# Sixty-four bytes ahead of the weights' slots, other places for act_hi and act_lo, and one buffer less

## What is computed

```python
hx = modulate(rms_norm(x, g_mix_pre), sh1, sc1)              # and hc, of the context
uf, ux, ug = split(hx @ w_in)                                # 1024 + 1024 + 1024
y = concat([fourier_mix(uf), (h_f + h_b) * gelu(ug)]) @ w_out   # h_f, h_b: gated scans over conv(ux)
x = x + gt1 * rms_norm(y, g_mix_post)
hx2 = modulate(rms_norm(x, g_ffn_pre), sh2, sc2)
up = depthwise_conv(hx2 @ w_up)                              # 2048 -> 2 * 5632
g, v = split(up)
x = x + gt2 * rms_norm((gelu(g) * v) @ w_down, g_ffn_post)
```

## Time and profile before

| | |
|---|---|
| median of 3 runs | 2106.05 us (2105.69 to 2107.88) |
| profiled execution, its own time | 2105.41 us |
| span of its trace | 2103.6 us |
| PE busy | 2071.2 us, 98% |
| granted TensorE clock, mean of the span | 0.996 |

### The profile page before, as it was taken

The page is one execution under the profiler, slowest core; times in us unless marked ns, Lnnn a source line. Parts: engine busy times, 40 slices in busy tenths (PEclk is TensorE's granted clock), DMA queues, the critical chain, the costliest instruction groups (busy, mean ns, idle before and its releaser), DMA issues.

```text
span 2103.6 us, 28297 instructions
## 1 busy us (share of the span) xinstructions
PE 2071.2 (98%) x11682; PEld 1772.5 (84%) x11682; DVE 1529.6 (73%) x2202; ACT 811.6 (39%) x1077; POOL 78.7 (4%) x145
## 2 busy tenths in 40 slices
PE   7999999999999999999999999999999999999998
PEld 4678887888777888888889898898988889888887
DVE  5567978876988975867767676676766758577577
ACT  5346577543323442423324233332333424233243
POOL 0000000001110000000000000000000000000002
PEclk9999999999999999999999999999999999999999
DMA  9953424434876523333333333334233333232343
GB/s 394 408 204 110 154 96 161 137 109 173 323 277 225 181 90 134 100 128 111 110 130 101 138 103 103 129 101 140 100 120 121 100 130 100 91 101 101 100 172 109
DMA packets 86193, 311.19 MB, mean 148 GB/s; under 512 B 9456, under 2 KB 13552, under 8 KB 84016
## 3 DMA queue, kind: packets, MB, share of 16 engines
q1 hardware_dynamic: 67824, 243.09, 32.7%
q0 software_dynamic: 17424, 65.50, 9.1%
q10 hardware_dynamic: 816, 0.79, 0.1%
HBM read 300.95 MB, written 8.39 MB: 147 GB/s over the span
## 4 chain that ended last, share of the span: by engine, by line
PE 80%; DVE 2%; ACT 1%; DMA 1%; issue 0%; DVEq 0%; ACTq 0%
PE bank L988 26%; PE bank L990 26%; PE bank L989 26%; DMA w_raw<-in_stream 1%; PE bank L1099 1%; DVE acc L2167 0%; PE bank L1284 0%; DVE w_lo L1532 0%; ACT w_hi L602 0%; PE bank L1313 0%; PE bank L1194 0%; DVE acc L2139 0%; ACT lru_u L698 0%; DVE cv L1544 0%; DVE x L2193 0%
## 5 line engine op out<-in xcount | busy, mean ns | idle before, releaser
L988 PE MATMUL bank<-h_hi,w_hi 128*128 128x512 f32 (+1 forms) x1968 | 711.2, 361 | 4.2 <-ACT y_lru L671 1.2
L989 PE MATMUL bank<-h_lo,w_hi 128*128 128x512 f32 (+1 forms) x1968 | 708.6, 360 | 0.0
L990 PE MATMUL bank<-h_hi,w_lo 128*128 128x512 f32 (+1 forms) x1968 | 707.2, 359 | 0.0
L1532 DVE TENSOR_TENSOR w_lo<-w_raw,w_hi 128x1024 fp32r<-128x1024 f32 x260 | 316.0, 1222 | 157.9 <-ACT w_hi L602 157.8
L988 PEld LDWEIGHTS bank<-h_hi,w_hi 128*128 128x128 f32 x1968 | 372.3, 189 | 63.6 <-issue 11.9
L602 ACT ACTIVATE w_hi<-w_raw 128x1024 fp32r<-128x1024 f32 x260 | 273.0, 1056 | 389.1 <-DMA w_raw<-in_stream 389.0
L990 PEld LDWEIGHTS bank<-h_hi,w_lo 128*128 128x128 f32 x1968 | 372.1, 189 | 56.6
L989 PEld LDWEIGHTS bank<-h_lo,w_hi 128*128 128x128 f32 x1968 | 372.3, 189 | 49.0
L988 PE MATMUL bank<-act_hi,w_hi 128*128 128x512 f32 (+1 forms) x688 | 265.0, 385 | 1.7 <-DVE acc L2139 1.5
L990 PE MATMUL bank<-act_hi,w_lo 128*128 128x512 f32 (+1 forms) x688 | 264.2, 384 | 0.0
L989 PE MATMUL bank<-act_lo,w_hi 128*128 128x512 f32 (+1 forms) x688 | 264.2, 384 | 0.0
(11 more groups left out here) (340 smaller groups left out, 2711.4 us busy)
## 6 DMA issues: line engine op xcount, KB each, us to landing
w_raw<-in_stream SPq DMA_DIRECT2D x340, 512.0 KB, 3.5
ada_raw<-in_adabg POOLq DMA_DIRECT2D x112, 512.0 KB, 4.3
ada_raw<-in_ada SPq DMA_DIRECT2D x64, 512.0 KB, 13.5
x<-in_x_t SPq DMA_DIRECT2D x4, 1024.0 KB, 8.4
acc<-in_adabg SPq DMA_DIRECT2D x8, 512.0 KB, 6.1
x<-in_x_t POOLq DMA_DIRECT2D x4, 1024.0 KB, 9.4
x_kept_d<-x SPq DMA_DIRECT2D x4, 1024.0 KB, 5.6
c<-in_ctx_t SPq DMA_DIRECT2D x2, 1024.0 KB, 14.3
```

The lines of the kernel that those rows point to most:

```text
L988: t.matmul(out, w, v, start=start, stop=False)
L989: t.matmul(out, w, v_l, start=False, stop=False)
L990: return t.matmul(out, w_l, v, start=False, stop=stop)
L1532: v.tensor_tensor(lo_unit(n), raw_unit(n), hi_unit(n).bitcast(F32), ALU.subtract).then_inc(lo_done, 1)
```

## The change

It allocates 64 unused bytes (`gap_to_weights`) behind `h_lo`; all tiles that follow from the left side move by 64 bytes. It makes `gap_to_act` 304 elements (1216 bytes) smaller, so that `act_hi` and `act_lo` start 1152 bytes lower than before, or 1216 bytes lower with respect to the weights' slots, which is 192 mod 1024. It drops the tile `ada_rows` (1024 bytes), so that `ada0_raw` still ends below the tiles on the right side, and copies the conditioning rows to `csq0[:, 0, :]`. No instruction is added or taken away, and no loop, shape or wait is changed. `h_hi` and `h_lo` stay where they are.

```diff
         x0, h_lo = twice(ctx, "x0", "h_lo", [P, KT, L])
+        sbuf(ctx, "gap_to_weights", [P, 16])
         w_raw, w_lo = twice(ctx, "w_raw", "w_lo", [P, RING, UNIT])
...
-                ada_rows = sbuf(s0, "ada_rows", [P, 2 * P])
+                ada_rows = csq0[:, 0, :]
...
-            sbuf(s, "gap_to_act", [P, 416])
+            sbuf(s, "gap_to_act", [P, 112])
...
-                a.activation(ada_rows[:, :], rows_bank(c)[:, 0:2 * P], ACT.Copy).then_inc(rows_copied, 1)
+                a.activation(ada_rows, rows_bank(c)[:, 0:2 * P], ACT.Copy).then_inc(rows_copied, 1)
```

## The result

The change makes the kernel slower: 2121.54 us (2119.70 to 2124.19, 3 runs) against 2106.05 us, ratio 1.0076 with a 95% interval of 1.0058 to 1.0094. I had forecast 2098 us, a small gain. It came out on the side of the rival *slower*, to which I had given 0.19, and past the upper end of my range, 2120 us. The profiled execution of the changed kernel took 2119.7 us with a span of 2117.9 us, 14.3 us more than before. In the changed file every line behind the new one has a number higher by one: `three` is L989 to L991.

A forecast was written before the change was run, and what follows sets the result against it. PE, busy 98% of the span, was taken to be bound by the distance between product starts. From the profiled 2105.41 us, 8.2 us less gave 2097.2, forecast as 2098 us; range 2070 to 2120 us for 8 in 10.

The forecast's parts named there:

- slower: 6192 products of `h` and `act` with 512 columns stay near 230 ns, 3.3 above 226.7: 20 us, 2126 us; chance 0.19.
- What bounds the kernel: PE is busy 98% of the span; the distance between starts of products decides, not what feeds PE.
- the surcharge of 13.3 ns a product: Distance between product starts beyond columns at 2.4 a ns, same for 256 and 512 columns; 143 us of the span.
- No cost from the shared rows, the DMA, ACT and DVE: Conditioning rows in `csq0` add no wait, bound 1 us; DMA, ACT and DVE keep their instructions and order: 0.
- The value for wide products: Products of `h` and `act` with 512 columns were forecast to gain 1.0 ns each, like those with 256.
- the mean of the three: Mean of `sums1` (-1.7 ns), `channel_mix` (-1.3) and `token_dft` (0): -1.0 ns for 8160 products, 8.2 us less.
- The value for narrow products: Products of `h` and `act` with 256 columns were forecast to gain 1.0 ns each, with bounds 0 and 1.7.
- the bound of 1.7 ns: Largest gain a product, from 18 products of `sums1` at 118.3 ns against 120.0; 13.9 us less for all 8160.
- The kinds whose phase stays: `hc`, `t` by slots and `weights_dft` keep their phase to the weights and should keep their distances.
- No change: Rival: the surcharge is the price of reading 128 columns of weights, addresses only shift it; 2106 us, chance 0.30.
- Much faster: Rival: weights and stream part for half the surcharge or more; 54 us less for 8160 products, 2052 us; chance 0.13.
- The page's rule: PE's port waits for no one, with separate read ports for moving operand and weights; addresses would not matter, 2106 us.

The follow-up runs named there:

- the streaming kernels: Two kernels without the layer, only streaming products at chosen phases of moving operand to weights; at phase 0, 512 columns took 226.7 ns a product.
- The control: Kernel before with the slots of the `seven_products` units put last and one load waiting later, but no shift within the slot: 2182.95 us, ratio 1.0362.

## Why the prediction was wrong

**What bounds the kernel, and what a change of addresses can touch.** Right. PE waits for nothing in the long window, and all of the difference is in the surcharge of 13.3 ns a product. With 20 ns for wide `h` products and about 9 for narrow ones it is the surcharge that moved.

**No cost from the shared rows, the DMA, ACT and DVE.** Right, and shown by the run with all tiles moved together, whose ratio is 1.0000.

**The value for wide products.** This is the step that failed: "I choose the mean of the three, -1.0 ns, for all 8160." The three rows were of narrow products, and I carried them over to the 6192 wide ones of `h` and `act`; what stood for it was that the surcharge at phase 0 is the same at both widths. The runs showed that the width decides the sign. Wide products paid 26.7 us more (22.7 for `h`, 4.0 for `act`), 4.3 ns each. The surcharge that is the same at both widths holds at phase 0 and not in general: at 64 bytes it is 15.5 ns for 512 columns and 6.7 or 11.1 for 256, at 448 bytes, the new phase of `h`, 20 for 512 and 6.7 or 11.1 for 256.

**The value for narrow products.** The sign was right, the size too small: 7.5 us for 1680 products of `h` are 4.5 ns each, above the bound of 1.7 ns. That bound came from short runs at other phases; at the new phase of `h` itself the streaming kernels have 117.8 or 113.3 ns, 2.2 or 6.7 below phase 0.

**The kinds whose phase stays.** I wrote that they should keep their distances. `t` by `w` kept its phase and gained 2.8 us. With the same addresses of `t` and weights but `h` back at phase 0 it gained nothing (the run with all tiles moved), so the phase of its `h` neighbours reaches over the turn. So "if products whose phase stays change as well, for then it is not the phase but the address itself" was a wrong test. The run with all tiles moved is the right one.

**The rivals.** *Slower* named the mechanism and the place: wide products never reach the settled 226.7 ns. Its price was 20 us for 6.2 thousand wide products and measured 26.7; it left out that narrow products gain, 11.4 us with `t`. Its evidence deserved more than 0.19: the only wide rows off the settled rhythm were all above it, and I had no wide row below it. *No change* leaned on `token_dft`, 24 products with two phases among them; no other row or run at a phase off 0 has exactly the surcharge of phase 0 at both widths. *Much faster* does occur for narrow products, 113.3 ns at 64 bytes, and nowhere for wide ones.

**The page's rule.** The Trainium skill, page "SBUF — State Buffer", section "SBUF: two separate sides", has PE's port wait for no one and two read ports on PE. As I read it, moving `act` alone would then change nothing. The trace has 43.96 us for 43.52, so that reading fails for two operands of one engine, and the measurement decides. What is behind it, in the memory, between memory and array, or in the array, no run here tells. They tell that it goes with the phase and the width, that phases 0, 256, 512 and 768 are alike, and that the phase alone doesn't fix every value.

## What to carry to other kernels

- A kernel that waits for nothing on PE can still be 0.3 to 1.2% off by where its tiles start. For products of 512 columns in this format, align moving operands and weights modulo 256 bytes; for 256 columns 64 bytes off, either way, was better by 2 to 7 ns a product. A gap that looks like waste may be what holds a phase: move partners together.
- Don't carry a price per instruction from one shape to another where its mechanism isn't known. Give such a price both signs, or sweep it by itself: one streaming kernel of 0.5 ms had the sign for both widths and named phase 0 as the best for wide products. Its values did not all carry over (233.3 ns at 320 bytes, and 229.0 for `act` in the kernel), so the kernel itself has the last word.
- When a rearrangement needs a later wait, run it without the intended effect as well. The control told that 77 us came from the rearrangement (55 of them stand in its trace as waits for `w_lo`) and not from the phases.

## What I had not expected of the hardware

- The distance between products depends on the phase of the two operands, from 256 bytes on with a period of 256, and the width decides the sign: at 64 bytes 384 columns pay the 13.3 ns of phase 0, 256 columns less, 512 more. 128 columns take 111.7 ns at every phase, nearly as long as 256 columns with 113.3 to 120.1.
- Narrow products at one and the same phase and address have two steady rhythms, 113.3 and 117.8 ns, and a run of 48 or of 192 keeps the one in which it settled within its first dozen.
- Even 16 bytes matter: 231.6 ns for wide products where phase 0 has 226.7, 116.6 for narrow ones where it has 120.0.
